# First chunk of three feed-forward blocks with channels on partitions, x entering by half quarters, and wide matmuls grouped ahead of narrow ones

## The reference

```python
def rms_norm(x, w):
    y = xf * lax.rsqrt(jnp.mean(xf * xf, axis=-1, keepdims=True) + NORM_EPS)
    return y * w

def swiglu_ffn(h, w_gate_up, w_down):       # 1024 -> 2 x 2816 -> 1024
    gate, up = jnp.split(h @ w_gate_up, 2, axis=-1)
    return (jax.nn.silu(gate) * up) @ w_down

for layer in range(2):
    h = h + 0.5 * swiglu_ffn(rms_norm(h, ffn1_norm[layer]), ...)   # f = 0, 2
    h = h + mixer(rms_norm(h, mix_norm[layer]))
    h = h + 0.5 * swiglu_ffn(rms_norm(h, ffn2_norm[layer]), ...)   # f = 1, 3
```

## Time and profile before

| | |
|---|---|
| runs | 1028.49, 1030.55, 1701.71 us |
| profiled execution | 1029.14 us |
| its span | 1027.4 us |
| granted TensorE clock | 0.999 |
| TensorE matmul busy | 1016.9 us, 99% of the span |
| VectorE, ScalarE busy | 675.4 us (66%), 569.1 us (55%) |

### The profile page before, as it was taken

How to read it: one execution, slowest core, us unless ns; L and a number is a source line. 1 busy time by engine, 2 the same in 40 slices (tenths; PEclk the granted TensorE clock), 3 DMA queues, 4 the chain that set the end, 5 groups by cost and what they waited for, 6 DMA issues and landing times.

```text
span 1027.4 us, 15453 instructions
## 1 busy us (share of the span) xinstructions
PE 1016.9 (99%) x5790; PEld 881.5 (86%) x5790; DVE 675.4 (66%) x1005; ACT 569.1 (55%) x907; POOL 60.3 (6%) x120
## 2 busy tenths in 40 slices
PE   8999999999999999999999999999999999999997
PEld 7888888887888888888888888999999988888886
DVE  5766765576566776635766764688597666776733
ACT  7645543457565654536545543577567655554532
POOL 0000000110000000000000000404205100000000
PEclk9999999999999999999999999999999999999999
DMA  9666465343346555563665465343242347556521
GB/s 322 214 208 200 163 245 201 138 165 109 99 130 228 172 186 216 212 199 102 196 213 191 166 243 205 118 155 123 83 144 83 124 144 231 179 176 219 213 87 41
DMA packets 124308, 175.81 MB, mean 171 GB/s; under 512 B 7360, under 2 KB 97760, under 8 KB 124256
## 3 DMA queue, kind: packets, MB, share of 16 engines
q1 hardware_dynamic: 121552, 172.77, 49.5%
q10 hardware_dynamic: 2704, 2.33, 0.7%
HBM read 174.02 MB, written 1.06 MB: 170 GB/s over the span
## 4 chain that ended last, share of the span: by engine, by line
PE 97%; DVE 1%; ACT 1%; DMA 1%; issue 0%; SPq 0%; ACTq 0%; DVEq 0%
PE bank L1761 29%; PE bank L1691 15%; PE bank L1693 15%; PE bank L1692 14%; PE bank L1763 14%; PE bank L2085 2%; PE bank L2079 2%; PE bank L1988 1%; PE bank L1712 1%; PE bank L1923 1%; PE bank L1954 1%; PE bank L1853 1%; DMA w_raw<-in_ffn_w_gate_up 1%; DVE x_sb L1184 0%; PE bank L2182 0%
## 5 line engine op out<-in xcount | busy, mean ns | idle before, releaser
L1761 PE MATMUL bank<-xT,w_hi 128*128 128x512 f32 x1280 | 444.9, 394 | 0.0
L1147 DVE TENSOR_TENSOR w_lo<-w_raw,w_hi 128x2048 fp32r<-128x2048 f32 x152 | 347.4, 2290 | 105.7 <-ACT w_hi L727 105.0
L727 ACT ACTIVATE w_hi<-w_raw 128x2048 fp32r<-128x2048 f32 x153 | 294.0, 1930 | 118.0 <-PE bank L1693 118.0
L1763 PE MATMUL bank<-xT,w_lo 128*128 128x256 f32 x1280 | 354.8, 277 | 0.0
L1761 PEld LDWEIGHTS bank<-xT,w_hi 128*128 128x128 f32 x1280 | 240.0, 188 | 55.7
L1763 PEld LDWEIGHTS bank<-xT,w_lo 128*128 128x128 f32 x1280 | 240.4, 188 | 0.1
L1691 PE MATMUL bank<-w_hi,hT_hi 128*128 128x512 f32 x352 | 137.5, 391 | 0.0
L1693 PE MATMUL bank<-w_hi,hT_lo 128*128 128x512 f32 x352 | 137.0, 389 | 0.0
L1692 PE MATMUL bank<-w_lo,hT_hi 128*128 128x512 f32 x352 | 137.0, 389 | 0.0
L793 ACT ACTIVATE silu_g<-bank 128x256 f32<-128x256 f32 x80 | 26.4, 382 | 175.4 <-PE bank L1763 175.4
L1234 DVE TENSOR_TENSOR silu_g<-bank,silu_g 128x256 f32<-128x256 f32 x80 | 30.2, 419 | 119.5 <-ACT silu_g L793 119.5
(11 more groups left out here) (312 smaller groups left out, 1218.7 us busy)
## 6 DMA issues: line engine op xcount, KB each, us to landing
w_raw<-in_ffn_w_gate_up SPq DMA_DIRECT2D x170, 512.0 KB, 4.6
w_raw<-in_ffn_w_down SPq DMA_DIRECT2D x88, 512.0 KB, 4.0
w_raw<-in_gdn_w_in SPq DMA_DIRECT2D x32, 512.0 KB, 4.4
w_raw<-in_attn_w_in SPq DMA_DIRECT2D x12, 512.0 KB, 4.1
w_raw<-in_attn_w_out SPq DMA_DIRECT2D x8, 512.0 KB, 3.7
w_raw<-in_gdn_w_out SPq DMA_DIRECT2D x8, 512.0 KB, 3.6
w_raw<-in_ffn_w_gate_up SPq DMA_DIRECT2D x12, 256.0 KB, 6.1
x_sb<-in_x SPq DMA_DIRECT2D x4, 256.0 KB, 5.4
```

The costliest lines, as they stand in the source:

```text
L727: act.activation(w_hi[u0 % RING][:], w_raw[u0 % RING][:], ACT.Copy).then_inc(hi_ready, 1)
L1147: dve.tensor_tensor(w_lo[u0 % RING][:], w_raw[u0 % RING][:], w_hi[u0 % RING][:].bitcast(F32), ALU.subtract).then_inc(split_ready, 1)
L1761: pe.matmul(banks[m][:], w[0], xT[:, kt, :, :].rearrange("p s n -> p (s n)"), start=(kt == 0), stop=False, skip_group_check=True)
L1763: z = pe.matmul(banks[m][:, SEQ:2 * SEQ], w[1], xT_hi[:, kt, :], start=False, stop=(kt == KT - 1), skip_group_check=True)
```

## The change

- `channel_step` (new) holds one step of `gate_chunk` in all four blocks: the four wide matmuls first, then the four narrow ones.
- `entered_chunk` (new) computes chunk 0 of blocks f = 1, 2, 3: channels on partitions, gate channels in bank 2 and up channels in bank 3, 4 blocks x 8 `kt` x 3 products = 96 matmuls of 256 columns. It waits for `early_lo` by `kt`. Transposes of the third and fourth quarter of x come after the first and second `kt`, and the two transposes for `rstd` before the last `kt`. The four transposes of `h` are gone in these blocks.
- ScalarE and VectorE do chunk 0 of these blocks on whole 128x512 tiles: multiply by `rstd_rows`, Silu, multiply by the up part, split. The loop covers chunks 1 to 10 in five rounds there; block 0 keeps its form.
- `enter` of the three blocks has the order of the DeltaNet mixer. Banks are the same in all blocks.
- `transposed_rstd` (new) takes the place of `rstd_in_rows` in the mixer: two transposes for two float32 matmuls with the identity.

```diff
-                if e == E_GDN:
+                if e in BY_HALVES:            # {2: 0, 3: 1, 4: 2, 5: 3}
                     for n in range(2):
                         residual(e, n, factor)
                     enter_lo(e, 0, range(2))
...
+                if f:                          # ScalarE, after root(RSTD_FFN[f])
+                    copy_rows(ROWS_FFN[f], ROWS_BANK)
+                    act.wait_ge(g_scaled, NCH * f)
+                    act.activation(silu_g[0][:], silu_g[0][:], ACT.Silu).then_inc(g_silu, 1)
+                    split_hi(u + 4)
+                    act.wait_ge(h_cols, NCH * f)
+                    act.activation(hT_hi[:, 0:BANK], h_row[0][:].rearrange("p m n -> p (m n)"),
+                                   ACT.Copy).then_inc(hT_hi_ready, 1)
+                    split_hi(u + 5)
...
+                if f:                          # VectorE
+                    dve.wait_ge(rows_ready, ROWS_FFN[f])
+                    dve.wait_ge(unit_done, u + 2)
+                    dve.tensor_tensor(silu_g[0][:], bank[FIRST_CHUNK[0]][:].rearrange("p (m n) -> p m n", m=2),
+                                      rstd_rows[:]..., ALU.mult).then_inc(g_scaled, 1)
+                    dve.wait_ge(g_silu, NCH * f)
+                    dve.scalar_tensor_tensor(h_row[0][:], bank[FIRST_CHUNK[1]][:]..., 0.5,
+                                             silu_g[0][:], ALU.mult, ALU.mult).then_inc(h_cols, 1)
+                    split_lo(u + 4)
+                    dve.wait_ge(hT_hi_ready, NCH * f + 1)
+                    dve.tensor_tensor(hT_lo[:, 0:BANK], ...).then_inc(hT_lo_ready, 1)
+                    split_lo(u + 5)
...
-                        for m in range(4):
-                            w = ring(u0, slice(q * BANK + m * P, q * BANK + (m + 1) * P))
-                            pe.matmul(banks[m][:], w[0], xT[:, kt, :, :].rearrange("p s n -> p (s n)"),
-                                      start=(kt == 0), stop=False, skip_group_check=True)
-                            z = pe.matmul(banks[m][:, SEQ:2 * SEQ], w[1], xT_hi[:, kt, :], start=False,
-                                          stop=(kt == KT - 1), skip_group_check=True)
+            def channel_step(u0, kt, banks):
+                for m in range(4):
+                    w = ring(u0, slice(kt % 4 * BANK + m * P, kt % 4 * BANK + (m + 1) * P))
+                    pe.matmul(banks[m][:], w[0], xT[:, kt, :, :].rearrange("p s n -> p (s n)"),
+                              start=(kt == 0), stop=False, skip_group_check=True)
+                for m in range(4):
+                    w = ring(u0, slice(kt % 4 * BANK + m * P, kt % 4 * BANK + (m + 1) * P))
+                    z = pe.matmul(banks[m][:, SEQ:2 * SEQ], w[1], xT_hi[:, kt, :], start=False,
+                                  stop=(kt == KT - 1), skip_group_check=True)
+                return z
+            def transposed_rstd(n, b):
+                pe.wait_ge(rstd_ready, n)
+                for t in range(TT):
+                    z = pe.transpose(bank[b][:, t * P:(t + 1) * P], rstd[:, t:t + 1].broadcast_to([P, P]), ident[:])
+                z.then_inc(rows_psum, 1)
+            def entered_chunk(f):
+                e, u = E_FFN[f], U_FFN[f]
+                for kh in range(2):
+                    wait_split(pe, u + kh)
+                    for q in range(4):
+                        if kh and q == 3:
+                            transposed_rstd(RSTD_FFN[f], ROWS_BANK)
+                        if q < 3:
+                            pe.wait_ge(early_lo, 6 * BY_HALVES[e] + 3 * kh + q + 1)
+                        else:
+                            pe.wait_ge(xT_lo_ready, 4 * e + 2 * kh + 2)
+                        kt = 4 * kh + q
+                        for m in range(4):
+                            z = products(bank[FIRST_CHUNK[m // 2]][:, m % 2 * SEQ:(m % 2 + 1) * SEQ],
+                                         ring(u + kh, slice(q * BANK + m * P, q * BANK + (m + 1) * P)),
+                                         (xT_hi[:, kt, :], xT_lo[:, kt, :]), ...)
+                        if q == 3:
+                            z.then_inc(unit_done, 1)
+                        elif kh == 0 and q < 2:
+                            enter(e, 2 + q)
+                pe.wait_ge(rows_ready, ROWS_FFN[f])
```

More of the change, by code:

```diff
@@ L437, in build, with rounds @@
         out_stored = sem("out_stored")
[L438 to L441 removed]
+        def rounds(eng, f, body):
+            if f == 0:
+                body(0)
+            with eng.Fori(1 if f == 0 else 0, (NCH - 1) // 2) as i:
                 body(i)
@@ L944, in _ @@
             root(RSTD_GDN)
-            act.wait_ge(rows_psum, ROWS_GDN)
-            act.activation(rstd_rows[:], bank[7][:, 0:TT * P].rearrange("p (t n) -> p t n", t=TT),
-                           ACT.Copy).then_inc(rows_ready, 1)
+            copy_rows(ROWS_GDN, 7)
             act.wait_ge(wba_zero, 1)
@@ L1757, in gate_chunk @@
                             wait_split(pe, u0)
+                        z = channel_step(u0, 4 * kh + q, banks)
+                    z.then_inc(unit_done, 1)
+                    if j == 1 and kh == 0 and not looped(i):
+                        first_transposes()
+            def channel_step(u0, kt, banks):
[8 more added lines that the diff above has]
+                return z
@@ L1765, in gate_chunk @@
-                    z.then_inc(unit_done, 1)
-                    if j == 1 and kh == 0 and not looped(i):
-                        first_transposes(f)
-            def first_transposes(f):
-                pe.wait_ge(rstd_ready, RSTD_FFN[f])
-                pe.wait_ge(h_ready, TT * (f + 1))
-                for t in range(TT):
-                    z = pe.transpose(bank[FIRST_CHUNK[f][0]][:, t * P:(t + 1) * P], rstd[:, t:t + 1].broadcast_to([P, P]),
-                                     ident[:])
-                z.then_inc(rows_psum, 1)
+                            z = products(bank[FIRST_CHUNK[m // 2]][:, m % 2 * SEQ:(m % 2 + 1) * SEQ],
+                                         ring(u + kh, slice(q * BANK + m * P, q * BANK + (m + 1) * P)),
+                                         (xT_hi[:, kt, :], xT_lo[:, kt, :]),
+                                         start=(kt == 0 and m % 2 == 0), stop=(kt == KT - 1), skip_group_check=True)
@@ L1811, in ffn @@
             def ffn(f, e_next):
-                for kh in range(2):
-                    in_unit(U_FFN[f] + kh, 0, kh, FIRST_CHUNK[f], E_FFN[f])
-                if f == 0:
+                if f:
+                    entered_chunk(f)
+                else:
+                    for kh in range(2):
+                        in_unit(kh, 0, kh, FIRST_CHUNK, E_FFN[0])
                     pe.wait_ge(conv_loaded, 16)
@@ L2007, in channel_unit @@
                         z.then_inc(unit_done, 1)
-            def rstd_in_rows():
-                pe.wait_ge(rstd_ready, RSTD_GDN)
-                for t in range(TT):
-                    z = pe.matmul(bank[7][:, t * P:(t + 1) * P], rstd[:, t:t + 1].broadcast_to([P, P]), ident[:],
-                                  start=True, stop=True)
-                z.then_inc(rows_psum, 1)
             def entered_channel_unit(u0, kh, banks):
```

122 lines of the change are left out of this document (68 added, 54 removed).

## The result

Seven runs of the changed kernel have a median of 1032.36 us (1032.17 to 1032.71). Seven of the kernel before have a median of 1028.69 us: six lie between 1028.44 and 1030.55, and one is 1701.71. Without that one the ratio is 1.0034, with a 95% interval from 1.0021 to 1.0046: slower by 0.34%, where the prediction had a little faster. The profiled execution took 1032.41 us, its span 1030.7 us, 3.3 more than the span before. The medians are 3.7 us apart, because the profiled execution of the kernel before (1029.14 us) was itself 0.45 us above the median of its seven runs.

What follows compares the result with a forecast made beforehand. TensorE, 99% busy at full clock, was taken to bound the kernel. Terms -0.9 + 2.0 - 2.3 - 0.2 = -1.4 us from the profiled 1029.14 us give 1027.8, stated as 1028 us, range 1019 to 1037.

Steps and rivals of the forecast that it cites:

- A: Steps of chunks 1 to 10: matmul costs are additive, 1388 ns a grouped step against 1390, so grouping gains nothing.
- The prediction's own sign of being wrong: A step more than 10 ns off, or an entry with a wait that the mixer's does not have.
- the middle: Grouped steps cost what the old ones did, giving 1028 us in all; chance 0.55.
- The rival of the slow beat: Grouped steps run at 353 ns a pair: 27 ns x 320 = 8.5 us, 1036.3 us in all; chance 0.2.
- The rival of the quicker steps: Grouped narrow matmuls take 115 ns and wide ones gain too: up to -9 us, 1019 us; chance 0.15.
- B: Entry of blocks 1, 2, 3: 0.23 us instead of 0.53 before chunk 0, -0.30 us each, -0.9 us.
- C: Chunk 0 of blocks 1, 2, 3 in narrow matmuls: 12.63 us against 11.95, +0.68 us each, +2.0 us.
- D: Chunk 1 of blocks 1, 2, 3 without transposes in it: -0.76 us each, -2.3 us.
- E: The mixer's rstd: two transposes for two float32 matmuls, -0.2 us.
- F: ScalarE and VectorE work for chunk 0: some 6.9 us, covered by chunk 1's 11.09 us, so no cost.

Runs made afterwards that it cites:

- e4_grouped_only: The kernel before with grouped steps alone (four wide, then four narrow), entries and chunk 0 as before; median 1033.52 us, ratio 1.004.
- e2_unit_runs: The changed kernel with a unit's 16 wide matmuls in a row, then its 16 narrow ones; median 1028.82 us, ratio 1.0.
- e8: The changed kernel, grouped by four, with two added transposes ahead of chunk 1 of blocks 1 to 3; one run, 1033.33 us.
- e1_alternating: The changed kernel with wide and narrow matmuls of a step alternating again, all else kept; median 1033.79 us, ratio 1.0043.
- run 320: Not a label of a run: the words belong to "a step that is run 320 times", the count of steps in the kernel.
- e13: The changed kernel with alternating steps and one added transpose ahead of chunk 1 of blocks 1 to 3; median 1027.48 us, ratio 0.9994.
- e6: The changed kernel with alternating steps and two added transposes ahead of chunk 1 of blocks 1 to 3; median 1027.87 us, ratio 0.9996.
- e14: Repeat of the changed kernel with alternating steps and two added transposes ahead of chunk 1 of blocks 1 to 3; median 1027.85 us, ratio 0.9995.
- e10: The changed kernel with alternating steps, rstd transposes moved right ahead of chunk 1 and four more added behind them; median 1028.63 us, ratio 1.0003.
- e3: The changed kernel with steps of two wide matmuls, then two narrow, and again; median 1029.43 us, ratio 1.0003.
- e9: The changed kernel with alternating steps, except the first step of odd chunks in blocks 1 to 3, by twos; median 1033.44 us, ratio 1.005.

## Why the prediction was wrong

- **A failed, and with it the direction.** "320 steps gain nothing" took two long streams as the price of runs of four. The step measured 1403 ns (11.227 us for eight) against 1387: 4.8 us in chunks 2 to 10 and 0.4 in three chunks 1, +5.2 us where the sum had 0. e4_grouped_only shows that this cost comes from the order alone. The prediction's own sign of being wrong, a step more than 10 ns off, was met. The step of the argument that failed is "the cost is additive to the accuracy of the rows, whatever stands beside what": 4 x 227 + 4 x 120 agreed with the old step in the sum alone (it was 4 x 231.7 + 4 x 114.9), and grouped by four the wide ones stay at 232 while the narrow ones rise to 118.5. With runs of 16 the matmuls do come near the stream prices (229 and 119, e2_unit_runs). Why each pattern has its spacing stays open. I had named "the grouped pattern itself stands nowhere in the trace" and still gave the middle the highest chance; behind each set of transposes the trace before showed several wide ones at 0.23 to 0.24 us until they came to 0.227, and I read that only as the cost of a restart.
- **The rival of the slow beat** had the sign, but not the mechanism: 16.7 ns a step, not 27, and no grouped kernel showed a second beat: chunks 2 to 10 took 11.227 us in the changed kernel, in e4 and in e8. Its time, 1036.3 us, was too high.
- **The rival of the quicker steps** took narrow matmuls at 115 ns as what grouping would bring. 115 was what they cost while alternating; grouped they cost more.
- **B was right**: the three entries gained 0.8 us where 0.9 was said (0.30 in block 2, whose rows were read, and 0.24 in each of the others).
- **C was right**: +1.95 us for chunk 0 against +2.0; rstd was written at 483.01 and wanted at 483.47, and TensorE did not wait.
- **D was right as a sum and wrong as an account.** -1.9 us, where -2.3 was said; the 0.134 us missing in each of the three chunks is term A's. But I counted the transposes in chunk 1 as a cost only. They are also what stood between the slow and the quick beat. With alternating steps, taking them out costs 10 chunks x 0.214 us in each of three blocks, 6.4 us: the entry alone makes the kernel 4.7 us slower (e1_alternating), not 1.4 faster. The change did not pay this, since none of the grouped kernels had a slow beat.
- **E was right**: the rstd transposes of the mixer, "x2" for "x4", and the mixer's stretch of the earlier trace rows is 0.2 us shorter.
- **F was right in the result**, but its chain had the table load between VectorE's two multiplies, where it did not stand. Timeline of ScalarE and VectorE, block 2 of the changed kernel: table load, Silu of chunk 0, and the last split that chunk 2 needs.

```profile
484.29 1.28 ACT L833 ACT_TABLE_LOAD   x1
486.14 0.63 ACT L833 ACTIVATE silu_g<-silu_g 128x512 f32<-128x512 f32 x1 [0.57 <-DVE silu_g L1308]
...
491.42 2.29 DVE L1163 TENSOR_TENSOR w_lo<-w_raw,w_hi 128x2048 fp32r<-128x2048 f32 x1
```

The table load began while TensorE was still in chunk 0 and ended before VectorE's first multiply did (486.11), and the last split ended at 493.7 us, 2.6 before chunk 2 began.
- **Range**: the time, 1032.36, lies inside 1019 to 1037 and within 2%. The direction was wrong. The base also hid a little of the error: the forecast was counted from an execution of 1029.14 us, 0.45 above the median of seven. From 1028.69 the same terms give 1027.3 us; the miss is then 5.1 us, and term A is all of it.

The sum with the measured A: 1029.14 - 1.4 + 5.2 = 1032.9 us; the profiled execution took 1032.41, with a first stage (to chunk 1 of block 0) 0.7 us shorter.

## What to carry to other kernels

A stream of matmuls of changing width may have more than one steady spacing, and which one a loop runs in can be set by what stands before it. Price a new order from the same pattern in a trace, not from streams of its parts, and when one stage is removed, compare the spacing of the stages behind it, not only its own time. Where TensorE is 99% busy, 16 ns in a step that is run 320 times are worth more than all waits of three entries.

## What the runs showed of the hardware that I had not expected

- Alternating 512- and 256-column fp32r matmuls at a granted clock of 0.998 to 0.999 ran at 347 or at 353 ns a pair, and kept either for 300 pairs, through a loop's back edges and all work on other engines.
- By run length the same 32 pairs take 11.093 or 11.307 (1), 11.147 (2), 11.227 (4), 11.173 (8) and 11.133 us (16).
- Versions with the quick beat had a few executions 1.9 to 2.3 us above the rest (1029.33 and 1029.79 beside a median of 1027.48 in e13; 1029.83 and 1030.0 beside 1027.87 in e6; 1029.86 beside 1027.85 in e14; 1030.6 beside 1028.63 in e10), and so had the kernel before (1030.55 beside 1028.69). In the 32 executions of the changed kernel, e2, e3 and e4, whose steps are all in groups, none is more than 0.7 us above its median. One block in the slow beat is worth 1.9 to 2.1 us. That these were such executions is argued from the size and from which kernels have them; none of them was profiled, and e9, whose block 0 has the quick beat, has one too, 2.2 us above its median.
